# Two low-part buffers and the split activations of the expert products moved by 32 bytes

## The reference

```python
logits = (h @ router_w + router_b)
top_vals, top_idx = lax.top_k(logits, TOP_K)          # 4 of 32 experts for each token
...
def expert_block(args):                                # 128 rows of one expert
    xb, e = args
    gu = xb @ w_gu[e] + b_gu[e]                        # 128 x 1024 @ 1024 x 2048
    gate, up = jnp.split(gu, 2, axis=-1)
    gate = jnp.minimum(gate, SWIGLU_LIMIT)
    up = jnp.clip(up, -SWIGLU_LIMIT, SWIGLU_LIMIT)
    glu = gate * jax.nn.sigmoid(SWIGLU_ALPHA * gate)
    return ((up + 1.0) * glu) @ w_down[e] + b_down[e]  # 128 x 1024 @ 1024 x 1024
```

## The kernel before

| buffer | begins at | modulo 512 |
|---|---|---|
| e_hi (4 parts of 8192 bytes) | 162,976 | 160 |
| e_lo[0], e_lo[1] | 195,744 and 203,936 | 160 |
| x_hi, x_lo | 212,128 and 216,224 | 160 |
| e_lo[2], e_lo[3] | 82,048 (the start of area) and 90,240 | 128 |
| act_hi, act_lo | 104,576 and 108,672 | 128 |

## Time and profile before

### The profile page before, as it was taken

The page is one execution under the profiler, slowest core; times in us unless marked ns, Lnnn a source line. Parts: engine busy times, 40 slices in busy tenths (PEclk is TensorE's granted clock), DMA queues, the critical chain, the costliest instruction groups (busy, mean ns, idle before and its releaser), DMA issues.

```text
span 1568.9 us, 21558 instructions
## 1 busy us (share of the span) xinstructions
PE 1485.3 (95%) x7059; PEld 1155.6 (74%) x7060; DVE 1247.9 (80%) x1119; ACT 1073.7 (68%) x1136; POOL 318.1 (20%) x262
## 2 busy tenths in 40 slices
PE   3999997999899999999999999999999999999993
PEld 1657874457688888888888888888888888888872
DVE  1476757156798899999999998999999999998992
ACT  4442347254788887777777888887777777888881
POOL 1000000301032222222222222222222222322221
PEclk9999998998899999999999999999999999999996
DMA  9555530245799999999999999999999999999964
GB/s 330 174 168 212 212 104 1 73 183 193 282 365 363 359 351 365 361 368 361 359 365 368 368 375 364 352 363 364 360 369 360 354 363 373 373 367 359 349 264 124
DMA packets 97663, 475.17 MB, mean 303 GB/s; under 512 B 26320, under 2 KB 36536, under 8 KB 45408
## 3 DMA queue, kind: packets, MB, share of 16 engines
q1 hardware_dynamic: 85120, 451.45, 74.9%
q0 software_dynamic: 12512, 23.31, 5.6%
HBM read 468.62 MB, written 23.67 MB: 314 GB/s over the span
## 4 chain that ended last, share of the span: by engine, by line
PE 91%; ACT 3%; DVE 2%; DMA 2%; issue 1%; SPq 1%; POOLq 0%; DVEq 0%; ACTq 0%; POOL 0%
PE bank L1460 15%; PE bank L1461 15%; PE bank L1462 15%; PE bank L1483 8%; PE bank L1484 7%; PE bank L1485 7%; PE bank L1307 4%; PE bank L1118 3%; PE bank L1119 3%; PE bank L1120 3%; PE bank L1441 2%; PE bank L1433 2%; PE bank L1075 1%; PE bank L1268 1%; PE bank L1454 1%
## 5 line engine op out<-in xcount | busy, mean ns | idle before, releaser
L1590 DVE TENSOR_TENSOR e_lo<-ring,e_hi 128x2048 fp32r<-128x2048 f32 x384 | 868.2, 2289 | 88.4 <-ACT e_hi L759 88.3
L759 ACT ACTIVATE e_hi<-ring 128x2048 fp32r<-128x2048 f32 x384 | 730.4, 1920 | 236.2 <-PE bank L1462 230.5
L1460 PE MATMUL bank<-e_hi,x_hi 128*128 128x512 f32 x1024 | 405.7, 396 | 2.7 <-DVE e_lo L1590 2.7
L1461 PE MATMUL bank<-e_lo,x_hi 128*128 128x512 f32 x1024 | 405.1, 396 | 0.0
L1462 PE MATMUL bank<-e_hi,x_lo 128*128 128x512 f32 x1024 | 403.3, 394 | 0.0
L1460 PEld LDWEIGHTS bank<-e_hi,x_hi 128*128 128x128 f32 x1024 | 193.5, 189 | 53.8 <-issue 7.2
L1462 PEld LDWEIGHTS bank<-e_hi,x_lo 128*128 128x128 f32 x1024 | 193.2, 189 | 42.0
L1461 PEld LDWEIGHTS bank<-e_lo,x_hi 128*128 128x128 f32 x1024 | 193.4, 189 | 41.3
L1483 PE MATMUL bank<-e_hi,act_hi 128*128 128x512 f32 x512 | 206.1, 403 | 0.5 <-DVE act_lo L1603 0.5
L1484 PE MATMUL bank<-e_lo,act_hi 128*128 128x512 f32 x512 | 202.5, 395 | 0.0
L1485 PE MATMUL bank<-e_hi,act_lo 128*128 128x512 f32 x512 | 202.2, 395 | 0.0
(11 more groups left out here) (237 smaller groups left out, 1547.6 us busy)
## 6 DMA issues: line engine op xcount, KB each, us to landing
ring<-in_w_gu SPq DMA_DIRECT2D x256, 1024.0 KB, 7.9
ring<-in_w_down SPq DMA_DIRECT2D x128, 1024.0 KB, 7.1
ring<-in_ada_w SPq DMA_DIRECT2D x24, 1024.0 KB, 9.0
ring<-in_w_in SPq DMA_DIRECT2D x9, 1024.0 KB, 7.0
ring<-in_w_o SPq DMA_DIRECT2D x4, 1024.0 KB, 6.5
ring<-in_w_in SPq DMA_DIRECT2D x10, 256.0 KB, 6.1
xs<-in_x SPq DMA_DIRECT2D x4, 512.0 KB, 5.3
xn_rows<-area POOLq DMA_DIRECT2D x4, 512.0 KB, 3.6
```

What stands on the lines that cost most here:

```text
L759: return nc.scalar.activation(dst, src, ACT.Copy, scale=scale)
L1460: pe.matmul(bank[b][:], x_hi[:, c, :], hi, start=False, stop=False)
L1461: pe.matmul(bank[b][:], x_hi[:, c, :], lo, start=False, stop=False)
L1590: tt(e_lo[c % PARTS][:], raw(period.raw_slot(c)), e_hi[:, c % PARTS, :].bitcast(F32), ALU.subtract).then_inc(lo_ready, 1)
```

## The change

Four buffers are moved by 32 bytes: `e_lo[2]` and `e_lo[3]` and the pair `act_hi`, `act_lo`. The new start is worked out from the address of `e_lo[0]`, so that its remainder modulo 512 is the same: (195,744 - 82,048) mod 512 = 32. After the change all four are at remainder 160, like the rest of the operands. No instruction, size, wait or order is changed.

```diff
         e_hi = sb("e_hi", [P, PARTS, SLOT], F32R)
-        e_lo_at = [nc.sbuf_base, nc.sbuf_base + 4 * SLOT, area_at, area_at + 4 * SLOT]
+        tail_at = area_at + (nc.sbuf_base - area_at) % 512
+        e_lo_at = [nc.sbuf_base, nc.sbuf_base + 4 * SLOT, tail_at, tail_at + 4 * SLOT]
         e_lo = [nc.alloc_sbuf_tensor_at(f"e_lo{n}", [P, SLOT], F32R, offset=at) for n, at in enumerate(e_lo_at)]
-        act_hi = nc.alloc_sbuf_tensor_at("act_hi", [P, KD, P], F32R, offset=area_at + 4 * 5632)
-        act_lo = nc.alloc_sbuf_tensor_at("act_lo", [P, KD, P], F32R, offset=area_at + 4 * 6656)
+        act_hi = nc.alloc_sbuf_tensor_at("act_hi", [P, KD, P], F32R, offset=tail_at + 4 * 5632)
+        act_lo = nc.alloc_sbuf_tensor_at("act_lo", [P, KD, P], F32R, offset=tail_at + 4 * 6656)
```

## The result

| | before | after |
|---|---|---|
| median | 1571.74 us (4 runs, 1569.62 to 1572.13) | 1557.01 us (4 runs, 1555.52 to 1558.42) |
| profiled execution, its span | 1570.96, 1568.9 us | 1555.52, 1553.4 us |
| one pass | 36.09 us | 35.61 us |

The ratio is 0.9909, with a 95% interval of 0.9892 to 0.9926: faster by 14.7 us by the medians, where 13.4 were forecast. A later set of 4 runs gave 1556.32 and 0.9905 (0.9888 to 0.9921).

A forecast was written before the change was run, and what follows sets the result against it. TensorE was taken to pace the expert loop. 31 passes of 0.43 us (0.22 gate-up, 0.23 down) plus 0.1 gave 13.4 us, so 1572.05 - 13.4 = 1558.6 us; range 1555.5 to 1565.5, some 0.87.

The forecast's parts named there:

- TensorE sets the pace, the others have room: Expert loop, 420 to 1510 us: TensorE busy throughout; ScalarE, VectorE and DMA follow it with room.
- Remainder, not region: Gate-up and down chunks: slow pace comes from operands' start addresses modulo 512, not from the memory area holding the buffers.
- (a): Gate-up product: e_lo[2], e_lo[3] to remainder 160 bring chunks 2, 3, 6, 7 to 2.72 us, gaining 0.22 us a pass.
- (b): Down product: act_hi, act_lo to 160; chunks 1 to 3 at 2.72 us, chunk 0 at 2.89, gaining 0.23 us a pass.
- The sum: Whole kernel: 31 passes of 0.43 us give 13.3, plus 0.1 for the last down product, 13.4 us.
- (c): Transposes and bias matmuls between products unchanged; ScalarE's and VectorE's writes to moved buffers cost nothing visible.
- (d): Moved buffers end 32 bytes further, over router weights' first columns and the first expert's slot table; no wait added.
- Only one product gains: Down product's pace has another reason, such as two result banks; only gate-up's 0.22 a pass, 1565.2 us; chance 0.05.
- Transfers as the bound: Expert loop: a DMA ceiling of 365 GB/s would limit the gain to 6 us, time 1566; chance 0.04.
- Slower by VectorE's writes: Gate-up chunks: VectorE's writes at the readers' remainder slow every chunk, 6.8 us lost, 1578.9 us; chance 0.03.
- No change: Whole kernel: region sets the pace, or the skill page's port rule holds; time 1572 us; chance 0.06.

The follow-up runs named there:

- the padding: Changed kernel plus 32 bytes before e_hi: expert operands, h_hi and h_lo at remainder 192, w_hi and w_lo still at 160; 1557.31 us, ratio 0.9907.

## Why the prediction was right, point by point

- **TensorE sets the pace, the others have room**: right. TensorE is busy for all of the settled stretch, 1047 us before and 1033 after, and ScalarE still waits only for it.
- **Remainder, not region**: right, and now shown. Moves by 32 and by 512 bytes both keep the buffers in the region where they were: the first gave the gain (0.9909), the second nothing (1.0003). And the padding kept the projection's region and slowed it from 227.0 to 233.3 ns.
- **(a), 0.22 us a pass**: 0.21 by the rows shown (22.15 to 21.94, from 948.85 and 940.98 to the transposes), 0.22 as the mean of 27 passes (22.158 to 21.937).
- **(b), 0.23 us a pass**: 0.25 (11.28 to 11.03). The value for chunks 1 to 3 was right to the nanosecond. Chunk 0 was mis-sized: set at 2.89 by gate-up's, it came out at 2.86, between that and the bound of 2.72.
- **The sum, 13.4 us**: 14.7 by the medians, 14.3 by the ratio. I took 0.43 where my own two terms gave 0.45, and the pass gained 0.48, nearly all of it in the two products: 0.221 and 0.254 as means of 27 passes, and 0.005 in the rows between them. So 0.43 was too low by 0.05: 0.02 by my own rounding down, 0.03 by chunk 0 of the down product, which gained 0.05 and not 0.02. 31 passes of 0.48 are 14.9. The profiled spans differ by 15.5; two executions of the changed kernel have their first settled pass at 442.40 and 444.67 us, so a us or two of that lies ahead of the loop and is noise.
- **(c), (d), nothing**: right; the splitting instructions kept their durations, and no wait appeared.
- **Rivals.** Only one product gains: fell; by the ratios the low parts alone give 0.4%, the activations alone 0.2%, both 0.9%. Transfers as the bound: fell; 368 GB/s on the mean, no wait for a load. Slower by VectorE's writes: fell; VectorE now writes all four low parts at remainder 160, and no chunk slowed. No change: fell. The page "SBUF — State Buffer" of the Trainium skill, section "Who interferes with whom", says that PE never waits on anyone and that its two read ports are independent. The runs don't fit with two ports that are independent, for these matmuls: 226.7 against 233.3 ns by the start addresses of TensorE's own operands relative to each other. That TensorE waits for another engine no run shows. The 16-byte lines of the same page, section "Specifications (TRN2)", don't give the bound either: a distance of 16 bytes costs 5.2 ns.

## What to carry to other kernels

Where float32r matmuls of 512 columns run back to back, each with a fresh stationary operand, read the pace from their starts, chunk by chunk: two paces in one loop at one clock are a sign of the operands, not of the schedule. Then compare the start addresses of all moving and stationary operands modulo 256; if one is out of step, pad it (here 32 bytes for 0.9% of the kernel). Bring all of them into step at once: one stationary operand of three out of step cost as much as all (233.3 ns), and moving the low parts while the split activations stayed made the down product slower. And measure it for other shapes first, for which it can go the other way.

## What the runs showed that I had not expected

- **Every distance tried costs, and the cost doesn't grow with it.** Gate-up pace with one low part off by 8, 16, 64, 128, 192, 224 and 256 bytes: 231.8, 232.0, 231.3, 232.7, 230.4, 231.1 and 226.7 ns (224 is the kernel before; the 16 were 16 beyond a multiple of 256). With the stationary operand off by 32 (act_lo alone), 64 or 224: 233.3; by 256: 226.7. No distance is better than 0.
- **The slow pace outlasts its cause.** Gate-up chunk 4 reads operands that are all in step in every kernel. It ran at 226.7 ns where the chunk ahead had its low part 224 off (before), but at 228.4 behind one 128 off, 230.2 behind one 16 off and 230.1 behind one 192 off. There its first 4 to 9 steps are slow and the others 227. So the operands of a matmul alone don't fix its pace; what came before counts too.
- **At 256 columns it is the other way round.** The projection has products in which the weights move, 256 columns at a time (there w_hi and w_lo move and h_hi and h_lo are stationary). TensorE's timeline, first the kernel before, where they agree, then the padded one, where they are 32 bytes apart:

```profile
168.92 0.28 PE L1119 MATMUL bank<-w_lo,h_hi 128*128 128x256 f32 x1
...
180.19 0.28 PE L1120 MATMUL bank<-w_hi,h_lo 128*128 128x256 f32 x1
```

```profile
170.85 0.28 PE L1121 MATMUL bank<-w_lo,h_hi 128*128 128x256 f32 x1
...
181.97 0.28 PE L1122 MATMUL bank<-w_hi,h_lo 128*128 128x256 f32 x1
```

95 matmuls, 94 steps: 11.27 us (119.9 ns) in step, 11.12 us (118.3 ns) out of step. So here agreement costs 1.6 ns. Over 384 such matmuls that is 0.6 us back from the 2.0 us that the wide ones lost, which leaves the 1.4 us by which the projection got longer; 3.5 were expected because these products were taken to lose too. In a median with a spread of 1.3 us (1556.84 to 1558.17) the 1.4 don't stand out. More than the width differs from the expert products: the moving operand is taken in two pieces of 128 columns. Which of the two turns the sign was not tested.
- **A product needs 6 to 11 matmuls to settle**, even in step, in one of a few fixed orders (its first starts are 341, 240, 235, 233, 236 ns apart, or 335, 231, 236, 228, 233; 335, 235, 233, 236, 224 and 337, 231, 231, 236, 228 were seen too). The order repeats from pass to pass, and it changes by edits that don't touch the product. What picks it stays open; it is worth 0.04 us a product.
- **What stays open.** Why a start address matters at all. The numbers fit with reads of the moving operand and of the next stationary one meeting somewhere in the memory, with a period of 256 bytes (only 256 and 512 were tried); but that is argued, not shown. Against the plainest form of it: 8 stationary columns (32 bytes) already bring the pace to 231.0, where 128 columns bring it to 233.3.
